# Linear attention: the value product taken over the far and the near score tile separately, instead of over their sum

## The reference

```python
b = jnp.cumsum(gc, axis=-2)
o_inter = jnp.einsum("bhld,bhdv->bhlv", qc * jnp.exp(b), s)
rel = b[:, :, :, None, :] - b[:, :, None, :, :]
decay = jnp.exp(jnp.where(tri[:, :, None], rel, -jnp.inf))
a = jnp.einsum("bhid,bhjd,bhijd->bhij", qc, kc, decay)
o = o_inter + jnp.einsum("bhij,bhjv->bhiv", a, vc)
```

## Time and profile before

| what | value |
| --- | --- |
| median of 3 runs | 2372.49 us (2372.45 to 2372.76) |
| the profiled execution, its own time | 2373.44 us |
| its span | 2371.6 us |
| TensorE busy | 98% |
| VectorE busy | 73% |
| ScalarE busy | 48% |
| GpSimd busy | 15% |

### The profile page before, as it was taken

How to read it: one execution, slowest core, us unless ns; L and a number is a source line. 1 busy time by engine, 2 the same in 40 slices (tenths; PEclk the granted TensorE clock), 3 DMA queues, 4 the chain that set the end, 5 groups by cost and what they waited for, 6 DMA issues and landing times. The chain is left out here.

```text
span 2371.6 us, 35832 instructions
## 1 busy us (share of the span) xinstructions
PE 2315.1 (98%) x13842; PEld 1892.3 (80%) x13842; DVE 1725.2 (73%) x2633; ACT 1130.5 (48%) x1962; POOL 352.4 (15%) x287
## 2 busy tenths in 40 slices
PE   7999999999999999999999999999999999999998
PEld 5655988888888569888879777888888889848998
DVE  3575799987575977999865236878999835487875
ACT  3575644442442766443324444565443325386663
POOL 0110311110200003111112004341111111002110
PEclk9999999999999999999999999999999999999999
DMA  9603555556233032555552421044555635304664
GB/s 316 208 1 106 178 167 162 154 160 195 86 98 98 19 107 80 168 155 165 170 170 79 120 77 36 2 151 134 159 156 162 203 93 133 116 24 141 180 183 129
DMA packets 449965, 310.88 MB, mean 131 GB/s; under 512 B 11954, under 2 KB 405858, under 8 KB 449540
## 3 DMA queue, kind: packets, MB, share of 16 engines
q1 hardware_dynamic: 447024, 307.03, 43.8%
q10 hardware_dynamic: 2772, 1.56, 0.2%
HBM read 307.50 MB, written 1.05 MB: 130 GB/s over the span
## 5 line engine op out<-in xcount | busy, mean ns | idle before, releaser
L1780 PE MATMUL bank<-h_hi,slab_hi 128*128 128x512 f32 (+1 forms) x2416 | 840.4, 348 | 6.9 <-ACT slab_hi L631 4.1
L1780 PE MATMUL bank<-h_lo,slab_hi 128*128 128x512 f32 (+1 forms) x2416 | 829.0, 343 | 0.0
L1780 PE MATMUL bank<-h_hi,slab_lo 128*128 128x512 f32 (+1 forms) x2416 | 829.0, 343 | 0.0
L1104 DVE TENSOR_TENSOR slab_lo<-slab_raw,slab_hi 128x1024 fp32r<-128x1024 f32 (+1 forms) x388 | 526.0, 1357 | 239.3 <-ACT slab_hi L631 238.0
L1780 PEld LDWEIGHTS bank<-h_hi,slab_hi 128*128 128x128 f32 x2416 | 458.1, 190 | 89.5 <-issue 25.3
L631 ACT ACTIVATE slab_hi<-slab_raw 128x1024 fp32r<-128x1024 f32 (+1 forms) x388 | 400.7, 1034 | 257.1 <-PE bank L1780 194.2
L1780 PEld LDWEIGHTS bank<-h_hi,slab_lo 128*128 128x128 f32 x2416 | 458.3, 190 | 53.7
L1780 PEld LDWEIGHTS bank<-h_lo,slab_hi 128*128 128x128 f32 x2416 | 458.4, 190 | 53.3 <-issue 1.0
L1078 ACT ACTIVATE conv<-bank,prm 128x512 f32<-128x512 f32 (+1 forms) x176 | 127.9, 727 | 445.8 <-PE bank L1780 445.8
L1129 DVE SCALAR_TENSOR_TENSOR mod_sum<-slab_raw,cond_wide,mod_sum 128x512 f32<-128x512 f32 x420 | 316.5, 811 | 0.0
L1780 PE MATMUL bank<-g_hi,slab_hi 128*128 128x512 f32 (+1 forms) x788 | 272.8, 346 | 0.0
(11 more groups left out here) (256 smaller groups left out, 2657.8 us busy)
## 6 DMA issues: line engine op xcount, KB each, us to landing
slab_raw<-in_ffn_w_up SPq DMA_DIRECT2D x176, 512.0 KB, 4.0
slab_raw<-in_mod_w SPq DMA_DIRECT2D x132, 512.0 KB, 4.5
slab_raw<-in_ffn_w_down SPq DMA_DIRECT2D x64, 512.0 KB, 3.8
slab_open<-in_mod_w SPq DMA_DIRECT2D x36, 512.0 KB, 7.4
slab_gap<-in_mod_w SPq DMA_DIRECT2D x24, 512.0 KB, 8.7
slab_raw<-in_ffn_w_down SPq DMA_DIRECT2D x32, 384.0 KB, 3.3
slab_raw<-in_b_w_qkv SPq DMA_DIRECT2D x24, 512.0 KB, 3.7
slab_raw<-in_c_w_in SPq DMA_DIRECT2D x24, 512.0 KB, 3.8
```

Source lines behind the costliest of these rows:

```text
L1104: nc.vector.tensor_tensor(wlo[slot][:, 0:w], raw[of][:, 0:w], whi[slot][:, 0:w].bitcast(f32), ALU.subtract).then_inc(s_lo, 1)
L1780: ins = mm(out, l, r, start=first and n == 0, stop=last and n == 2, skip_group_check=parted)
```

## The change

VectorE's addition of the two tiles and its semaphore go. `place_near` ends with the spread, and before it overwrites `spread[p]` it now waits until `output` of the unit before has read it. `output` waits for `far_copied` and `spread` in place of `scores`, and takes the product of the values with each tile, one after the other into the same PSUM region.

```diff
 def place_near(u):
     for p in range(2):
         dve.wait_ge(S["reduced"], 2 * u + p + 1)
         if u:
-            dve.wait_ge(S["scores"], 2 * (u - 1) + p + 1)
+            dve.wait_ge(S["o_full"], 2 * (u - 1) + p + 1)
         nc.vector.tensor_tensor(spread[p][:], near[p][:].unsqueeze(1).broadcast_to([P, P // TILE, TILE]),
                                 diagonal[:], ALU.mult).then_inc(S["spread"], 1)
-    for p in range(2):
-        dve.wait_ge(S["far_copied"], 2 * u + p + 1)
-        dve.wait_ge(S["spread"], 2 * u + p + 1)
-        nc.vector.tensor_tensor(scores[p][:].rearrange("p (b i) -> p b i", i=TILE),
-                                scores[p][:].rearrange("p (b i) -> p b i", i=TILE), spread[p][:], ALU.add
-                                ).then_inc(S["scores"], 1)
...
-                    pe.wait_ge(S["scores"], 2 * u + p + 1)
+                    pe.wait_ge(S["far_copied"], 2 * u + p + 1)
+                    pe.wait_ge(S["spread"], 2 * u + p + 1)
...
                         mm(bank[4 + v][:, cs], vals[:, vc], scores[p][:], start=first, stop=False, skip_group_check=True)
+                        mm(bank[4 + v][:, cs], vals[:, vc], spread[p][:].rearrange("p b i -> p (b i)"), start=False,
+                           stop=False, skip_group_check=True)
```

More of the change, by code:

```diff
@@ L376, in build_program @@
             "k_turned", "end_full", "end_exped", "k_end", "g_hi", "g_lo", "sums", "decay", "q_prod", "k_prod", "q_dec", "edge",
-            "far_cleared", "score_full", "far_copied", "masked", "reduced", "spread", "scores", "update_full", "state", "o_full", "squared",
+            "far_cleared", "score_full", "far_copied", "masked", "reduced", "spread", "update_full", "state", "o_full", "squared",
             "o_gated", "ss_full", "rs_ready", "o_normed", "o_hi", "o_lo", "v_full")}
```

## The result

The changed kernel takes 2380.35 us (median of 7 runs, 2378.9 to 2383.03), the kernel before 2372.76 us (median of 7, 2372.03 to 2376.62). The ratio is 1.0029, with a 95% interval of 1.002 to 1.0038; the forecast was 2379.3 us and +0.29%. (The forecast added its 6.8 us to 2372.49 us, the median of the three runs known then.)

A forecast was written before the change was run, and what follows sets the result against it. TensorE, busy 98%, was taken to bound the kernel, in a chain with VectorE's `state` and `q_part`. Products 7.0 us less 0.2 gained at the last unit give +6.8 on 2372.49, so 2379.3 us; range 2376.0 to 2382.2.

The forecast's parts named there:

- What bounds the kernel: In the loop, a chain alternates between TensorE and VectorE through `state` and `q_part`; the add stands in no piece of it.
- The product's price: On TensorE in the loop, 32 added value products at 0.22 us each cost 7.0 us.
- the dearer 0.33 us: Rival: each added product costs 0.33 us, as the pair behind small products does; +10.4 us, 2382.9 us; chance 0.08.
- Nothing is hidden: TensorE's six waits for `q_part`, 5.4 us, take up none of the added products; all 7.0 us count.
- The last unit: At the end of the loop, TensorE no longer waits for the last pair of adds; 0.2 us gained, bounds 0 and 0.4.
- The new waits: VectorE's wait for `o_full` before the spread and one more TensorE wait per output cost 0, at most 0.8 us.
- Behind the loop: Work after the loop cannot win time back, since the load queue stands still; all that comes later shifts.
- the cover: VectorE's idle time before `o_head` and `masked`, 13.2 us, hides the other 14 adds, so removing them gains nothing.
- The growth of VectorE's waits: Sign: VectorE's waits before `o_head` and `masked` grow from 13.2 us by most of 5.4 + 6.2.

The follow-up runs named there:

- the second set of products: Changed kernel with the product with the near tile taken twice: 2386.85 us, against 2372.44 us for the kernel before; head 27.22 us.
- Neither: Changed kernel without the product with the near tile, so neither that product nor the add: 2372.35 us, ratio 1.0 to the kernel before.
- Add twice: Kernel before with VectorE's additions of the two tiles done twice: 2373.58 us, ratio 1.0005 to the kernel before.
- the moved reduction: Kernel before with VectorE's `reduce_near` moved behind the `q_part` of `q = 1`: 2370.17 us, ratio 0.9988 to the kernel before.

## Why the prediction was right

The medians moved by 7.6 us where 6.8 was forecast. The loop's own account has 6.9, and the 0.7 us between the two is within the scatter of the runs, so the sum was right by its terms and not by luck.

- **What bounds the kernel.** TensorE and VectorE in turns, VectorE's part of it being `state`, the reduction, `o_head` and `q_part`, not the add. Tested: removing the add leaves the head at 23.65 us, moving the reduction shortens it by 0.7 us and moving one `o_head` by another 0.06. That `state` and `q_part` belong to it is read from the chain alone.
- **The product's price.** 0.22 us each, 7.0 us in all. Between the marks +6.91 us for 32 products less 0.24; per head 1.78 to 1.80 us for 8, which is 0.223 to 0.225 us each. The record's duration of 275 ns and the dearer 0.33 us did not apply: the chain shows the new pair at 0.22 us in every place. The estimate from the Trainium skill ("FP8 and Floating Point Precision", TensorE Precision Notes, four passes, and "TensorE: Matmul & The Clock Gate", Back-to-back issue gap, some 81 ns each) was 10.4 us; the measurement decides against it.
- **Nothing is hidden.** Right, and it was the step most worth testing: the waits stayed at 5.4 us, and the second set of products cost as much as the first.
- **The last unit.** 0.2 us gained. Measured from the last product of `out_begin(0)` to the second of `out_begin(1)`: 3.35 us before (1537.31 to 1540.66), 4.03 after (1542.79 to 1546.82). Four products should add 0.89 and it is 0.68: 0.21 us gained. "Neither", without add and product, takes 13.87 us for the last stretch between two `squares_sum` where the kernel before takes 14.11: 0.24 us.
- **The new waits.** No cost seen: the first output of a unit follows the exponents with no gap, as before.
- **Behind the loop.** Nothing was won back: from the last `squares_sum` to the end of the span it is 828.5 us before, 828.4 us after, and 828.4 to 828.8 us in every other run.
- **Too loose a step: the cover.** I wrote that the 13.2 us of VectorE's waits hide the add. Those are the waits that turned longer, but they are not the cover. What had to stay on time was the `q_part` of `q = 2` behind the add, with 0.5 us to spare in the units with `half = 0`. "Add twice" used 0.41 us of it and a head showed nothing; the moved reduction used more than it, and TensorE waits 0.68 us there. Had the change come to a kernel in that order, the add would have been worth 0.76 us in each of the two heads where `head_lo` stands there too, and a few tenths at the ends, 1.9 us in all (loop 94.23 us with the add, 92.29 without), against the product's 7. That the add was free here was half a microsecond of margin, which the prediction had not looked at.
- **The growth of VectorE's waits.** "Most of" 11.6 us was forecast, 8.5 us came. A part of the freed time lies before `head_normed` (L1540 before, L1534 after), whose wait for ScalarE's `rstd` grew from 2.2 to 3.5 us, and some went into longer instructions. Kernel before, then changed kernel, in the same unit:

```profile
1493.39 1.09 DVE L1515 TENSOR_TENSOR scores<-scores,spread 128x128 f32<-128x128 f32 x2
1494.40 1.28 DVE L1544 TENSOR_TENSOR h_lo<-o_head,h_hi 128x512 fp32r<-128x512 f32 x2
...
1494.92 0.48 DVE L1510 TENSOR_TENSOR spread<-near,diagonal 128x128 f32<-128x128 f32 x2
1495.32 1.89 DVE L1538 TENSOR_TENSOR h_lo<-o_head,h_hi 128x512 fp32r<-128x512 f32 x2
```

The hold-up that the add took in the kernel before (1.09 us for a pair, where 0.48 is usual) has passed to its follower `h_lo`, 1.89 us where it took 1.28. In both kernels GpSimd's `k_part` runs beside the one that is held up:

```profile
1493.22 0.91 POOL L1742 TENSOR_TENSOR k_part<-qk,decay 128x256 f32<-128x256 f32 x1 [0.44 <-ACT decay L896]
...
1495.15 0.90 POOL L1736 TENSOR_TENSOR k_part<-qk,decay 128x256 f32<-128x256 f32 x1 [0.44 <-ACT decay L896]
```

Taking the add away did not take GpSimd's instruction away, and it met the next one. It fits the shared port of the Trainium skill ("SBUF — State Buffer", Who interferes with whom), by which a VectorE instruction with two inputs in SBUF contends with a GpSimd instruction that reads SBUF. That GpSimd is the cause is read from these times; no run moved or removed its work.

One slip in the working: 2378.0 less 1.8 is 2376.2, not the 2376.0 of the range's low end. Nothing hangs on it.

## What to carry to other kernels

Replacing a VectorE step by a TensorE product pays only if the step is on the way to something that TensorE waits for; a high busy share of VectorE does not say so, the releaser of TensorE's waits does. Work added to an engine that waits is free only if it stands between the event that starts the other engine's answer and the wait for that answer, so look for the operand that is ready earliest (here the far tile) and put its product there. And before trading work between engines, look at the order on the engine that answers: moving calls behind the one that is awaited gained 5 us here and cost no instruction.

## What the runs showed that I had not expected

The length of one head repeats to 0.02 us within an execution, and between kernels that have the same order on the engines that matter (23.65 us with the add, without it and with it twice), while whole runs scatter by several microseconds. Parts of the order that do not touch each other add up: 1.78 to 1.80 us for the products in every order in which TensorE had the same waits with and without them. And hold-ups between two-input VectorE instructions and their neighbours wander: 0.6 us moved from the add to `h_lo` with the change, and three `q_part` in the same place took 1.15 us before, 1.69 with the add twice and 2.23 with the reduction moved. The longer ones among them run beside a `k_part` on GpSimd.
